# Opening loads reordered and moved to SyncE, first two low parts moved to VectorE, decay tables built at the end of a step, and layer 1's tables loaded in layer 0's down stage

## The chip, the cores and the metric

The kernel runs on one core of a Trainium2 chip. The metric is the device time of one execution in microseconds (us). Three runs of the kernel before took 2464.4, 2457.11 and 2462.2 us, a median of 2462.2 us.

## The reference, cut to what matters

Two blocks are applied one after the other to x of shape (1, 512, 1024), in fp32. The first has two layers, and each layer computes:

```python
proj = x @ w_in[i]                      # q, k, v of both attentions, gates
ya = neighbourhood_attention(q_na, k_na, v_na, na_rpb[i])        # softmax over a 2D window
yb = bidirectional_retention(q_r, k_r, v_r, g_r, decay_f, decay_b)  # decay_in = exp(log_g * |i-j|)
merged = sigmoid(gate_a) * (ya @ w_branch_a[i]) + sigmoid(gate_b) * (yb @ w_branch_b[i])
x = layer_norm(ALPHA * x + merged @ w_out[i], ...)
ffn = conv_glu_ffn(x, w_up[i], conv_w[i], conv_b[i], w_down[i])
ple = sigmoid(x @ w_ple_gate[i]) * (p[i] @ w_ple_proj[i])
x = layer_norm(ALPHA * x + ffn + ple, ...)
```

The second block (one layer, called the mixer here) has a pooling and a state-space branch and a gated feed-forward part. Neither the change nor the rows below touch it, but for small parameters that are loaded at the start.

## The kernel before, in words

**Products in three passes.** Every fp32 operand of a large product is split into a high part (rounded to the matmul's type) and a low part (the rest). Each product is three matmuls: high x high, low x high, high x low (`passes`, line 730 is its matmul). So TensorE does three matmuls of 128x512 per tile of 128x128 weights.

**The weight stream.** All weights lie in one array of units, 8 tiles (512 KB) each, in the order of use. A ring of four slots holds them. For each unit SyncE (SP) loads `stage` (line 355, it waits for `lo_done` of the slot's last user), ScalarE (ACT) copies it to `w_hi` (line 1164 in `round_ahead`, three units ahead of the product, or line 1479 for the first three units), GpSimd (POOL) subtracts to get `w_lo` (line 400). TensorE (PE) waits for `lo_done` in `take_unit` and counts `unit_used` when it is through.

**The opening.** SP issues unit 0, then x in four loads of two feature tiles each (with unit 1 after the first of them), then units 2 and 3. ACT's queue issues first ident, pick, lnp, convp, decay (all counted in `params_in`), lam, log_dt and mpar (lines 1471 to 1475), and then makes `w_hi` and `xh`; VectorE (DVE) makes `xl` (line 2056); POOL makes all low parts. PE waits for all five of `params_in` (line 1140) ahead of its first matmul. After `xh`, ACT forms the logarithm of the decay rates (`decay_a`, lines 1492 to 1496, with two small steps of DVE at 2059 and 2061).

**Layers.** In each layer L, the loads of rope (cosines and sines), delta (position differences) and masks go out from ACT's queue (lines 1499 to 1501) once all of `xl` is made, since they share their place in SBUF with the up stage's buffers `conv_a` and `conv_b`. DVE waits for all three (`tables_in`, line 2065) ahead of its first step. Then come four attention steps, a loop in each engine's program. A step (`attention`) has 12 units: units 0 and 1 together (`first_units`), unit 2, scores of the window attention, unit 3, more scores, and so on. On DVE a step begins with the decay table of its head: lines 1545 to 1550, two tensor_scalar and one tensor_tensor of 128x896, counted in `dterm`; ACT makes its exponential at line 1216, and DVE uses `d_tab` late in the step. Behind the table on DVE come `na_low` (line 1607), which subtracts the rounded queries and keys from PSUM and so frees the two banks of units 0 and 1, `mask_scores` (bias at 1558, masks at 1566), `normalise` (1586) and `rotate` (1593 to 1600, rope). ACT begins a step by issuing the bias load (1207) and with `round_ahead(0)` and the copy of the queries (1181). PE's unit 2 needs the bank of unit 0, so it waits for `na_q_lo`.

After attention come branches, the output projection, a norm, the per-layer-embedding part, up (44 units), down (22 units; `residual_down` adds each of 8 results to z at line 1806) and a second norm (`norm(L, 1)`: mean on PE, centring on DVE at 1729, squares on ACT at 1297). POOL also computes, between its low parts in layer 0's attention, a long series of small steps for the mixer's eigenvalues, beginning with `growth_and_angle`, which waits for lam and log_dt.

The waits that hold a step's begin on DVE, word for word:

```python
            dve.wait_ge(mpar_in, 16)
            for L in range(DEPTH):
                dve.wait_ge(tables_in, L * 48 + 48)
                stand(dve, dve_passed)
                with dve.Fori(0, 4) as t:
                    attention(L, t)
```

## Time and profile before

| | us |
|---|---|
| median of three runs | 2462.2 |
| runs | 2457.11 to 2464.4 |
| the profiled execution, its own time | 2459.35 |
| its span, first to last instruction | 2457.5 |
| PE busy | 2365.7 (96% of the span) |
| POOL busy | 1121.7 (46%) |
| ACT busy | 976.9 (40%) |
| DVE busy | 962.2 (39%) |

The span is cut into stretches in which a different engine ends the wait. The chain of waits says which work ended last; the timeline gives start, length, engine, line and operation of each instruction, and in brackets how long its engine had been idle and what ended that. Of TensorE, the windows give a granted clock: 1.00 is 2.4 GHz, 0.50 is 1.2 GHz, and values between are a mix over the window. A matmul row's length overlaps the next one's, so rates are read from starts.

### The profile page before, as it was taken

How to read it: one execution, taken by the hardware profiler on the slowest of the kernel's cores; microseconds unless marked ns; L12 is line 12 of the kernel's file. 1: busy time of each engine (PE TensorE's matmuls, PEld its weight loads, DVE VectorE, ACT ScalarE, POOL GpSimd, SP SyncE). 2: the span in 40 equal slices, each digit the busy share in tenths (PEclk: the TensorE clock that was granted, in tenths of full speed). 3: DMA queues.
4: the chain of work that ended last, by engine and by line, in shares of the span. 5: the costliest groups of instructions: out<-in, count | busy, mean ns of one | idle time of the engine just before them, and what ended most of it. 6: DMA issues, size and time to landing. Idle time of an engine off the chain costs nothing.

```text
span 2457.5 us, 32539 instructions
## 1 busy us (share of the span) xinstructions
PE 2365.7 (96%) x11792; PEld 1947.2 (79%) x11792; DVE 962.2 (39%) x1487; ACT 976.9 (40%) x1318; POOL 1121.7 (46%) x686
## 2 busy tenths in 40 slices
PE   7999999999999998999999999999999889999998
PEld 5877888878888886788888887888888667888886
DVE  6454453343433203543543234444365594111101
ACT  4343343343555414333434224455521524444321
POOL 5677333444444453233332553444455564444442
PEclk9999999999999998999999999999999899999999
DMA  5212222223232322122222322233233112222331
GB/s 184 75 51 75 83 68 94 95 65 111 90 102 92 105 95 92 61 75 75 75 76 70 103 96 79 89 96 102 94 112 103 52 35 77 94 95 93 103 98 56
DMA packets 60990, 214.12 MB, mean 87 GB/s; under 512 B 7168, under 2 KB 7424, under 8 KB 60928
## 3 DMA queue, kind: packets, MB, share of 16 engines
q1 hardware_dynamic: 56896, 203.45, 25.3%
q10 hardware_dynamic: 4032, 9.81, 1.2%
q8 instruction: 44, 0.72, 0.1%
q14 instruction: 18, 0.15, 0.0%
HBM read 211.13 MB, written 2.10 MB: 87 GB/s over the span
## 4 chain that ended last, share of the span: by engine, by line
PE 87%; DVE 6%; ACT 3%; issue 2%; DMA 1%; POOL 1%; SPq 0%; DVEq 0%; ACTq 0%; POOLq 0%
PE psum L730 83%; PE psum L839 2%; DVE states L1932 1%; DVE s_t L1586 1%; PE psum L826 1%; ACT z L1314 1%; ACT s_t L1194 1%; ACT xh L1313 1%; DMA masks<-in_masks 0%; DMA stage<-in_w 0%; DVE z L1729 0%; PE psum L926 0%; PE psum L941 0%; PE psum L1042 0%; POOL rstd L609 0%
## 5 line engine op out<-in xcount | busy, mean ns | idle before, releaser
L400 POOL TENSOR_TENSOR w_lo<-stage,w_hi 128x1024 fp32r<-128x1024 f32 x380 | 925.8, 2444 | 1269.5 <-ACT w_hi L1164 1258.1
L730 PE MATMUL psum<-xh,w_hi 128*128 128x512 f32 x1888 | 747.2, 396 | 30.5 <-DVE xl L2056 13.3
L730 PE MATMUL psum<-xl,w_hi 128*128 128x512 f32 x1888 | 741.4, 393 | 0.0
L730 PE MATMUL psum<-xh,w_lo 128*128 128x512 f32 x1888 | 740.9, 392 | 0.0
L1164 ACT ACTIVATE w_hi<-stage 128x1024 fp32r<-128x1024 f32 x377 | 396.6, 1053 | 353.5 <-PE psum L730 352.7
L730 PEld LDWEIGHTS psum<-xh,w_hi 128*128 128x128 f32 x1888 | 358.6, 190 | 113.0 <-issue 20.6
L730 PEld LDWEIGHTS psum<-xh,w_lo 128*128 128x128 f32 x1888 | 358.4, 190 | 76.0
L730 PEld LDWEIGHTS psum<-xl,w_hi 128*128 128x128 f32 x1888 | 359.2, 190 | 72.9
L730 PE MATMUL psum<-g_hi,w_hi 128*128 128x512 f32 x528 | 205.4, 389 | 0.0
L730 PE MATMUL psum<-g_lo,w_hi 128*128 128x512 f32 x528 | 205.4, 389 | 0.0
L730 PE MATMUL psum<-g_hi,w_lo 128*128 128x512 f32 x528 | 205.4, 389 | 0.0
L730 PEld LDWEIGHTS psum<-g_hi,w_hi 128*128 128x128 f32 x528 | 99.1, 188 | 20.7
L730 PEld LDWEIGHTS psum<-g_lo,w_hi 128*128 128x128 f32 x528 | 99.1, 188 | 20.5
L730 PEld LDWEIGHTS psum<-g_hi,w_lo 128*128 128x128 f32 x528 | 99.1, 188 | 20.4
L1339 ACT ACTIVATE conv_b<-psum,convp 128x512 f32<-128x512 f32 x44 | 34.3, 779 | 145.6 <-PE psum L730 145.6
L1784 DVE SCALAR_TENSOR_TENSOR conv_b<-psum,convp,conv_b 128x511 f32<-128x511 f32 x44 | 33.0, 749 | 149.2 <-ACT conv_b L1339 149.2
L2030 DVE TENSOR_TENSOR hidden<-psum,silu 128x512 f32<-128x512 f32 x22 | 15.2, 691 | 183.7 <-PE psum L730 183.7
L730 PE MATMUL psum<-w_hi,xh 128*128 128x256 f32 x256 | 74.5, 291 | 4.6 <-DVE r_tmp L1594 4.6
L730 PE MATMUL psum<-merged_p,w_hi 128*128 128x512 f32 x256 | 78.8, 389 | 0.0
L730 PE MATMUL psum<-w_lo,xh 128*128 128x256 f32 x256 | 73.2, 286 | 0.0
L730 PE MATMUL psum<-w_hi,xl 128*128 128x256 f32 x256 | 73.1, 285 | 0.0
L1806 DVE TENSOR_TENSOR z<-z,psum 128x512 f32<-128x512 f32 x16 | 11.0, 687 | 154.6 <-PE psum L730 154.6
(354 smaller groups left out, 3260.3 us busy)
## 6 DMA issues: line engine op xcount, KB each, us to landing
stage<-in_w SPq DMA_DIRECT2D x380, 512.0 KB, 3.5
bias<-in_bias ACTq DMA_DIRECT2D x8, 384.0 KB, 3.1
z<-in_x SPq DMA_DIRECT2D x4, 512.0 KB, 8.5
out_x<-out_t SPq DMA_DIRECT2D x4, 512.0 KB, 2.7
masks<-in_masks ACTq DMA_DIRECT2D x2, 576.0 KB, 5.8
rope<-in_rope ACTq DMA_DIRECT2D x2, 512.0 KB, 3.8
p_raw<-in_p ACTq DMA_DIRECT2D x2, 512.0 KB, 3.6
delta<-in_delta ACTq DMA_DIRECT2D x2, 448.0 KB, 4.5
```

The source lines that it names most:

```text
L400: pool.tensor_tensor(w_lo[s][:, :, :], stage[s][:, :, :], w_hi[s][:, :, :].bitcast(F32), ALU.subtract).then_inc(lo_done, 1)
L730: mm = pe.matmul(dst, lhs[i], rhs[j], start=start and n == 0, stop=stop and n == 2)
L826: mm = pe.transpose(T_BANK[i % 2][:, b * P:(b + 1) * P], s_t[:, i, b * P:(b + 1) * P], ident[:, :])
L839: mm = pe.matmul(dst, na_v[:, j - 1 + b, r0:r0 + NA_DH], pt[:, i % 2, b * P:(b + 1) * P], start=b == bs[0], stop=b == bs[-1])
L1164: act.activation(w_hi[s][:, :, :], stage[s][:, :, :], ACT.Copy).then_inc(hi_done, 1)
L1194: act.activation(s, s, ACT.Exp, bias=row_nmax[:, i:i + 1], accum_out=row_sum[:, i:i + 1])\
L1313: act.activation(xh[:, k, :], p_sig[k % 4][:, :], ACT.Identity, bias=b).then_inc(x_hi, 1)
L1314: act.activation(z[:, k, :], p_sig[k % 4][:, :], ACT.Identity, bias=b).then_inc(x_ready, 1)
L1339: act.activation(buf[c][:, :], U_BANK[half][:, :], ACT.Identity, scale=convp[:, bass.ds(L, 1), 1, ch].rearrange("p l c -> p (l c)"), bias= ...
L1586: dve.tensor_scalar(s, s, row_inv[:, i:i + 1], None, ALU.mult).then_inc(p_ready, 1)
L1784: dve.scalar_tensor_tensor(out=y[:, 1:T], in0=ps[:, 0:T - 1], scalar=tap(0), in1=y[:, 1:T], op0=ALU.mult, op1=ALU.add).then_inc(conv_left, 1)
L1932: dve.tensor_tensor_scan(x[:, m, :], st[:, 4, 4 * q + m:4 * q + m + 1].to_broadcast([P, NB]), x[:, m, :], 0.0, ALU.mult, ALU.add).then_inc ...
```

## The change

SP now issues every opening load, in this order: unit 0, x tile 0, x tile 1, unit 1, x tiles 2-3, 4-5, 6-7, unit 2, decay, delta, unit 3, ident, pick, masks, rope, lam, log_dt, mpar, lnp, convp. ACT's queue issues none at the start; ACT instead runs a one-element copy as soon as two constants are set. The low parts of units 0 and 1 are made by DVE in place of POOL. The one semaphore for all tables becomes several (delta, masks, cosines and sines, ident with pick, decay), each waited for where its data is used; PE no longer waits for parameters at its start, and ACT waits for lnp and convp ahead of its first attention step. The decay table is made by a function `decay_table`: for layer 0's first step ahead of the loop, for later steps at the end of the step before, and for layer 1's first step inside layer 0's down stage, into a buffer of its own over `xl`, from where ACT copies it to `d_tab` at the start of the norm. DVE's loop over steps runs three times and the fourth step is written out behind it. Layer 1's delta, masks and rope are loaded by ACT's queue at the start of layer 0's down stage, once the last low part of the up stage's result (`g_lo`) is there.

```diff
@@ -174,6 +174,8 @@
         d_tab = place("d_tab", [P, 7 * P])
+        d_next = place("d_next", [P, 7 * P], offset=z_at - 4096)
+        d_next_tmp = place("d_next_tmp", [P, 7 * P], offset=z_at - 8192)
@@ -354,13 +357,29 @@
+            def load_x(i, first, end):
+                sp.dma_start(z[:, first:end, :], a["x"][:, first:end, :]).then_inc(x_in[i], 16)
+
             load(0, 0)
-            for h in range(4):
-                sp.dma_start(z[:, 2 * h:2 * h + 2, :], a["x"][:, 2 * h:2 * h + 2, :]).then_inc(x_in[h], 16)
-                if h == 0:
-                    load(1, 1)
+            load_x(0, 0, 1)
+            load_x(1, 1, 2)
+            load(1, 1)
+            for h in range(1, 4):
+                load_x(1 + h, 2 * h, 2 * h + 2)
             load(2, 2)
+            sp.dma_start(decay[:], a["decay"]).then_inc(decay_in, 16)
+            sp.dma_start(delta[:, :], a["delta"]).then_inc(delta_in, 16)
             load(3, 3)
+            for dst, src in ((ident, "ident"), (pick, "pick")):
+                sp.dma_start(dst[:], a[src]).then_inc(pe_params_in, 16)
+            sp.dma_start(masks[:, :, :], a["masks"]).then_inc(masks_in, 16)
+            sp.dma_start(rope[:, :, :], a["rope"]).then_inc(cos_sin_in, 16)
+            sp.dma_start(lam[:, :, :], a["lam"]).then_inc(lam_in, 16)
+            sp.dma_start(dt[:, 0, :], a["log_dt"]).then_inc(lam_in, 16)
+            sp.dma_start(mpar[:, :], a["mpar"]).then_inc(mpar_in, 16)
+            for dst, src in ((lnp, "lnp"), (convp, "convp")):
+                sp.dma_start(dst[:], a[src]).then_inc(params_in, 16)
+
@@ -581,7 +600,8 @@
-            low_parts(0, 4)
+            pool.wait_ge(lo_done, 2)
+            low_parts(2, 4)
@@ -811,6 +831,7 @@
                     pe.wait_ge(o_norm, it * 4 + 4)
+                    pe.wait_ge(pe_params_in, 32)
@@ -1137,8 +1158,7 @@
             pe.sem_inc(unit_used, 1)
-            pe.wait_ge(params_in, 16 * 5)
-            pe.wait_ge(consts_set, 3)
+            pe.wait_ge(consts_set, 4)
@@ -1213,6 +1233,8 @@
                 act.wait_ge(dterm, it * 3 + 3)
+                if L:
+                    act.wait_ge(dtab_moved, L)
@@ -1290,6 +1312,10 @@
                 to_mixer = n == DEPTH * 2 - 1
+                if which and not to_mixer:
+                    act.wait_ge(dterm, (L * 4 + 4) * 3 + 3)
+                    act.wait_ge(mean_done, n + 1)
+                    act.activation(d_tab[:, :], d_next[:, :], ACT.Copy).then_inc(dtab_moved, 1)
@@ -1468,11 +1494,8 @@
             act.sem_inc(bank_free[1], 1)
-            for dst, src in ((ident, "ident"), (pick, "pick"), (lnp, "lnp"), (convp, "convp"), (decay, "decay")):
-                act.dma_start(dst[:], a[src]).then_inc(params_in, 16)
-            act.dma_start(lam[:, :, :], a["lam"]).then_inc(lam_in, 16)
-            act.dma_start(dt[:, 0, :], a["log_dt"]).then_inc(lam_in, 16)
-            act.dma_start(mpar[:, :], a["mpar"]).then_inc(mpar_in, 16)
+            act.wait_ge(consts_set, 2)
+            act.activation(warm[:, :], ln_eps[:, :], ACT.Copy)
@@ -1480,14 +1503,14 @@
             for k in range(KT):
-                if k % 2 == 0:
-                    act.wait_ge(x_in[k // 2], 16)
+                if k < 2 or k % 2 == 0:
+                    act.wait_ge(x_in[k if k < 2 else 1 + k // 2], 16)
                 act.activation(xh[:, k, :], z[:, k, :], ACT.Copy).then_inc(x_hi, 1)
-                if k == 1:
+                if k == 0:
-            act.wait_ge(params_in, 16 * 5)
+            act.wait_ge(decay_in, 16)
@@ -1496,9 +1519,8 @@
                 act.wait_ge(x_lo, (L * 2 + 1) * KT)
-                act.dma_start(rope[:, :, :], a["rope"]).then_inc(tables_in, 16)
-                act.dma_start(delta[:, :], a["delta"]).then_inc(tables_in, 16)
-                act.dma_start(masks[:, :, :], a["masks"]).then_inc(tables_in, 16)
+                if L == 0:
+                    act.wait_ge(params_in, 32)
@@ -1518,6 +1540,11 @@
                     act.dma_start(c_st[:], a["c_st"]).then_inc(c_in, 16)
+                else:
+                    act.wait_ge(g_lo_s, (L + 1) * FT)
+                    act.dma_start(delta[:, :], a["delta"]).then_inc(delta_in, 16)
+                    act.dma_start(masks[:, :, :], a["masks"]).then_inc(masks_in, 16)
+                    act.dma_start(rope[:, :, :], a["rope"]).then_inc(cos_sin_in, 16)
@@ -1533,14 +1560,7 @@
-            def attention(L, t):
-                it = L * 4 + t
-                ui, ri = t * 12, t * 6
-
-                def after_score(n):
-
-                    return s_free[n % 2], it * 6 + (n // 2 + 2)
-
+            def decay_table(it, d_tab, d_tmp):
@@ -1548,6 +1568,15 @@
                 dve.tensor_tensor(d_tab[:, :], d_tab[:, :], d_tmp[:, :], ALU.subtract).then_inc(dterm, 1)
+
+            def attention(L, t, last=False):
+                it = L * 4 + t
+                ui, ri = t * 12, t * 6
+
+                def after_score(n):
+
+                    return s_free[n % 2], it * 6 + (n // 2 + 2)
+
@@ -1612,9 +1641,11 @@
                 na_low(1, na_k, 1.0)
+                dve.wait_ge(masks_in, L * 16 + 16)
                 mask_scores(1)
+                dve.wait_ge(cos_sin_in, L * 16 + 16)
@@ -1676,6 +1707,8 @@
                                       sg[:, f, :], ALU.mult).then_inc(ot_read, 1)
+                if not last:
+                    decay_table(it + 1, d_tab, d_tmp)
@@ -1804,6 +1837,9 @@
                     dve.tensor_tensor(z[:, m, :], z[:, m, :], U_BANK[m % 2][:, :], ALU.add).then_inc(bank_free[m % 2], 1)
+                    if L < DEPTH - 1 and m == 1:
+                        dve.wait_ge(delta_in, L * 16 + 32)
+                        decay_table(L * 4 + 4, d_next, d_next_tmp)
@@ -2047,11 +2083,20 @@
             dve.sem_inc(o_norm, 4)
+            dve.memset(ln_eps[:, :], LN_EPS).then_inc(consts_set, 1)
+            dve.memset(warm[:, :], 0.0).then_inc(consts_set, 1)
             dve.memset(mean_w[:, :], 1.0 / D).then_inc(consts_set, 1)
-            dve.memset(ln_eps[:, :], LN_EPS).then_inc(consts_set, 1)
             dve.memset(rms_eps[:, :], RMS_EPS).then_inc(rms_set, 1)
+
+            def first_low(n):
+                dve.wait_ge(hi_done, n + 1)
+                dve.tensor_tensor(w_lo[n][:, :, :], stage[n][:, :, :], w_hi[n][:, :, :].bitcast(F32), ALU.subtract).then_inc(lo_done, 1)
+
+            first_low(0)
             for k in range(KT):
+                if k == 1:
+                    first_low(1)
@@ -2060,15 +2105,18 @@
             dve.wait_ge(decay_step, 5)
-            dve.wait_ge(mpar_in, 16)
             for L in range(DEPTH):
-                dve.wait_ge(tables_in, L * 48 + 48)
                 stand(dve, dve_passed)
-                with dve.Fori(0, 4) as t:
+                if L == 0:
+                    dve.wait_ge(delta_in, 16)
+                    decay_table(0, d_tab, d_tmp)
+                with dve.Fori(0, 3) as t:
                     attention(L, t)
+                attention(L, 3, last=True)
                     branches(L, i)
+                dve.wait_ge(mpar_in, 16)
```

Left out of it: the semaphores that are declared, and unchanged lines.

## Rows read from the trace of the kernel before

**Rows 1.** The page, chain that ended last: shares of the span by engine.

```profile
PE 87%; DVE 6%; ACT 3%; issue 2%; DMA 1%; POOL 1%; SPq 0%; DVEq 0%; ACTq 0%; POOLq 0%
```

**Rows 2.** The chain of waits in order of time: start us, us, what.

```profile
27.61 6.81 PE psum L730 x30
...
973.79 5.54 DMA masks<-in_masks
...
987.29 8.84 PE psum L730 x30
```

**Rows 3.** Timeline at the start of layer 1.

```profile
971.21 1.63 DVE L1740 SCALAR_TENSOR_TENSOR xl<-p_sig,lnp,xh 128x512 fp32r<-128x512 f32 x2
...
974.57 0.35 ACTq L1207 DMA_DIRECT2D bias<-in_bias  x1
...
977.33 0.58 ACT L1181 ACTIVATE na_q<-psum 128x512 fp32r<-128x512 f32 x1
...
979.91 2.72 DVE L1547 TENSOR_SCALAR d_tmp<-delta,small 128x896 f32<-128x896 f32 x1
...
987.29 0.79 PE L730 MATMUL psum<-xh,w_hi 128*128 128x512 f32 x1 [10.25 <-DVE na_q_lo L1607]
```

**Rows 4.** Timeline of the opening: start us, us, engine line, work xcount [idle before <-releaser].

```profile
2.27 0.62 ACTq L1472 DMA_DIRECT2D convp<-in_convp  x1
...
2.92 0.52 ACTq L1472 DMA_DIRECT2D decay<-in_decay  x1
...
6.40 1.06 ACT L1479 ACTIVATE w_hi<-stage 128x1024 fp32r<-128x1024 f32 x1
...
13.29 0.77 PE L730 MATMUL psum<-xh,w_hi 128*128 128x512 f32 x1 [13.29 <-DVE xl L2056]
...
18.63 0.37 ACTq L1207 DMA_DIRECT2D bias<-in_bias  x1
...
24.09 0.20 DVE L1545 COPY small<-decay 128x2 f32 x1 [4.81 <-DMA masks<-in_masks]
...
25.07 0.60 ACT L1181 ACTIVATE na_q<-psum 128x512 fp32r<-128x512 f32 x1 [3.55 <-PE psum L730]
...
25.66 1.09 DVE L1550 TENSOR_TENSOR d_tab<-d_tab,d_tmp 128x896 f32<-128x896 f32 x1
...
26.68 0.88 DVE L1607 SCALAR_TENSOR_TENSOR na_q_lo<-psum,na_q 128x128 fp32r<-128x128 f32 x4
...
27.61 0.50 PE L730 MATMUL psum<-xh,w_hi 128*128 128x512 f32 x1 [0.53 <-DVE na_q_lo L1607]
```

**Rows 5.** DMA issues, whole kernel: what, queue, count, size, median us to landing.

```profile
stage<-in_w SPq DMA_DIRECT2D x380, 512.0 KB, 3.5
...
convp<-in_convp ACTq DMA_DIRECT2D x1, 176.0 KB, 9.2
...
decay<-in_decay ACTq DMA_DIRECT2D x1, 8.0 KB, 9.9
```

**Rows 6.** Windows of the opening: us, busy us of five engines, PEclk, DMA share, GB/s.

```profile
8.00:18.50 10.50, 5.21 (x12) 4.13 (x13) 9.15 (x9) 7.88 (x13) 6.83 (x3) 1.00 1.05 386
...
18.60:27.00 8.40, 8.40 (x37) 6.66 (x35) 3.49 (x8) 3.89 (x4) 5.34 (x8) 1.00 0.93 342
```

**Rows 7.** Timeline of layer 0's down stage and of the norm behind it.

```profile
835.94 1.99 ACT L1164 ACTIVATE w_hi<-stage 128x1024 fp32r<-128x1024 f32 x2
...
860.25 0.69 DVE L1806 TENSOR_TENSOR z<-z,psum 128x512 f32<-128x512 f32 x1 [14.28 <-PE psum L730]
...
952.63 1.82 ACT L1297 ACTIVATE sq<-z 128x512 f32<-128x512 f32 x3 [6.95 <-DVE z L1729]
```

**Rows 8.** Windows over three of the eight steps' softmax stretches (first, fifth, last).

```profile
46.00:62.00 16.00, 15.45 (x78) 13.22 (x79) 14.86 (x27) 6.49 (x15) 7.85 (x5) 0.79 0.20 67
...
1005.00:1020.00 15.00, 14.02 (x92) 12.25 (x90) 14.39 (x27) 6.83 (x16) 5.43 (x3) 1.00 0.22 72
...
1277.00:1292.00 15.00, 14.01 (x65) 11.52 (x64) 13.31 (x27) 6.68 (x17) 3.38 (x3) 0.77 0.21 70
```

More of the change, by code:

```diff
@@ L267, in build @@
         params_in = sem("params_in")
-        x_in = [sem(f"x_in{i}") for i in range(4)]
+        x_in = [sem(f"x_in{i}") for i in range(5)]
         consts_set = sem("consts_set")
@@ L271, in build @@
         decay_step = sem("decay_step")
-        tables_in = sem("tables_in")
+        delta_in, masks_in, cos_sin_in = sem("delta_in"), sem("masks_in"), sem("cos_sin_in")
+        pe_params_in, decay_in = sem("ident_and_pick_in"), sem("decay_in")
         bias_in = sem("bias_in")
@@ L276, in build @@
         vt_done, v_ready = sem("v_turned"), sem("v_ready")
-        dterm_copy = sem("decay_rates_copied")
+        dterm_copy, dtab_moved = sem("decay_rates_copied"), sem("decay_table_moved")
         dterm, dtab_ready = sem("decay_terms"), sem("decay_table_ready")
```

## The prediction, made before the changed kernel ran

> **What bounds the kernel now.** I read the chain of waits first. PE carries 87% of the span [rows 1], so time can only come from places where PE waits or runs at the lower of its two clock levels. In order of time the chain leaves PE for a long piece of DMA twice, and layer 1's piece is the load of the masks, 5.54 us, behind which a group of 30 matmuls takes 8.84 us; the same group takes 6.81 us at 27.61 [rows 2]. So a matmul costs 6.81/30 = 0.227 us at 2.4 GHz, and the group at 987.29 lost 2.03 us to 1.2 GHz after a pause.
>
> Then I read the timeline at both places. In layer 1, PE ends its first pair of units at 987.29 - 10.25 = 977.04 and stands for 10.25 us until DVE's `na_q_lo` frees the bank [rows 3]. ACT had the queries ready at 977.33, but DVE first waited for masks (973.79 + 5.54 = 979.3) and then made the decay table, whose first operation took 2.72 us with POOL at work. In layer 0 the same wait on DVE lasted 4.81 us, but PE lost only 0.53 us by it, since its first pair ended at 27.61 - 0.53 = 27.08; there the loss is in front: the first matmul is at 13.29, although `w_hi` of unit 0 was begun at 6.40 [rows 4]. The release is put down to `xl`, but the last of the five parameters, decay, landed at 2.92 + 9.9 = 12.8 [rows 4, 5], and that is what PE waited for. The opening's DMA runs at 386 and 342 GB/s with a busy share near 1 [rows 6]: it is bandwidth-bound.
>
> **Layer 1's tables, the main term.** The three issues on ACT go; with them the bias load is issued at about 972.9, when the last `xl` is done (971.21 + 1.63 = 972.8), not 974.57. From that issue to the query copy it was 977.33 - 974.57 = 2.76 us, so the copy comes at 975.7. PE's unit 0 is by then through (nine matmuls before 977.04, 975.0). The copy is 0.58; from the start of `na_q_lo` to PE's matmul it was 27.61 - 26.68 = 0.93 [rows 4]. With 0.05 between, unit 2 starts at 977.25 instead of 987.29: 10.04 us. The pause is now 0.2 us, so the clock stays up: 2.03 more. Sum 12.07. Masks and bias are needed only after unit 2.
>
> Price of the move. In the down stage ACT's wait for `g_lo` and three issues (0.35 to 0.6 each, as ACT's row of 0.62 for convp [rows 4]) put off `w_hi` at 835.94 by up to 2 us; three units of 24 x 0.227 = 5.4 us lie between it and its use, so PE covers it. DVE's table comes behind the addition at 860.25, with 14.28 us of idle time before each such addition [rows 7]; even at 2.72 for each tensor_scalar, and 1.09 for the third [rows 3, 4], it is 6.7 us and is hidden; without that cover it would cost 6.7. The 2.72 is what DVE pays beside POOL's subtraction. The Trainium skill, GPSIMD Engine Reference, Specifications, says that GpSimd's SBUF interfaces are shared with VectorE, against instructions in a two-port mode or with two SBUF inputs; the trace agrees for this table, and by that rule the copies at the opening are safe only because POOL is idle then. ACT's copy of the table, between 0.9 and 1.06 us (a 128x1024 copy [rows 4]), begins when the mean is done, 0.7 before the first square at 952.63 could start: the squares are put off by about 0.2 us, bounds 0 and 1.1.
>
> **The opening.** Unit 0 alone would land 3.5 us after issue at 0.73, at 4.2; I take 4.5 (upper bound 6.4, where its copy started [rows 4]). ACT's table load is out of the way by then. Copy 1.06, low part on DVE 1.25 (1.09 for 896 columns [rows 4], scaled to 1024), `xl` 0.7: PE's first three matmuls at 7.5. Two x tiles and unit 1, 1.05 MB at 386 GB/s, land at 7.2; copy 8.3, low part 9.5, next `xl` 10.2. The first pair took 27.08 - 13.29 = 13.8 us; with the break of 10.2 - 8.8 = 1.4 it ends at 22.7, 4.4 earlier. (The clock column says 1.00 there, but 48 matmuls at 0.227 would be 10.9; the starts show the lower level at first.)
>
> But ACT now waits for lnp and convp, the last of 20 loads on SP's queue, ahead of its bias load and its next `w_hi`. All 6.66 MB lie before it: 6.14 MB behind unit 0, at 386 to 342 GB/s 15.9 to 18.0 us, landing at 20.4 to 22.5 [rows 6]; I take 21.5. Then 0.3 into the loop, 2.76 to the query copy, 0.63 and 0.93 as above: unit 2 starts at 26.1 instead of 27.61. Gain 1.5; bounds 2.6 and, if convp lands at 23, 0. DVE's first table is done by then: log rates after unit 2's copy, about 17.5, and 2.9 of work. PE then idles 3.4 us between 22.7 and 26.1, and may run the next unit at the lower level: up to 2.0 lost, the size seen in layer 1. Against it DVE's softmax part of this step may escape POOL's low parts, up to 2 us gained. I take both together as zero. Everything that makes POOL start later (it gets lam later, and `w_hi` 3 later) is covered by PE's need of unit 4 only some 20 us on.
>
> **Steps.** The table at a step's end stands at the same place in DVE's order as at the next step's start: nothing. Waits added inside the steps (masks, cosines on DVE, ident on PE) are satisfied; at 0.02 to 0.07 each on the path, 16 of them cost 0.3 to 1.1; I take 0.5.
>
> **Sum.** 12.07 + 1.5 - 0.2 - 0.5 = 12.9 us. Against the profiled execution's own 2459.35 that is 2446.5; against the median, 2.85 higher, 2449.3. The mean of the four times known (three runs and the profiled one) is 2460.8, which gives 2447.9, my forecast. A measurement of this kernel can tell about 0.3% (7.4 us) from no change.
>
> **The clock as an unknown.** Behind each step's softmax PE pauses for some us; the granted clock over the eight stretches is 0.79 in the first, 1.00 in the fifth and 0.77 in the last [rows 8]. (1 - clock) x length is the time lost: 3.4, 0 and 3.4 in these. Since the change shifts all phases, each stretch may be drawn anew, so the fifth may lose 3.4 and the others gain. I take zero, +-3 for the range.
>
> **Rivals.**
> A. Small loads hold the queue. convp landed at 2.27 + 9.2 = 11.5 and decay, of 8 KB, at 12.8: 1.3 us for almost no bytes [rows 4, 5]. That was with a second queue taking turns; if it also holds on one queue, four such loads (decay, log_dt, mpar, lnp) add 5.2 us in place of the 1.1 that I left: convp at 25.6, unit 2 at 30.2, a loss of 2.6 instead of 1.5 gained, and 2.0 for the clock after 7.5 us of pause. 2447.9 + 6.1 = 2454.0. The Trainium skill, DMA: Bandwidth & Descriptors, Rules for kernel authors, says of transfers under 64 KB that one pays mostly overhead, which is this rival; no row shows it for one queue alone.
> B. The next wait takes the place. The load that ends ahead of unit 2 in layer 1 is not masks but ACT's order, or the stretches fall to the lower clock: if all eight lose 3.4, against about 13.5 now (mean 1.7), 13.7 is given back and the result is 2461.6, no change. For it: half the stretches show it now. Against it: all eight would have to.
> C. Slower. DVE's fourth step is written out, so its code is fetched afresh in both layers. If DVE must wait for its instructions, each time for a load as long as a landing here (3.5 us for one on a free queue [rows 5]), four times in each of two copies, while PE waits on it, that is 28 us: 2476. It decides above four such waits in all (12.9/3.5). Nothing in DVE's waits now shows one, and its straight-line code in the down stage and norms runs without any.
> D. The opening gives more (convp early, softmax free of POOL, clock kept): 3 to 4 us, 2444.
> E. The change doesn't do what it says: layer 1's wait stays since the tables come late. They have over 100 us between the down stage's start and use, so hardly.
>
> **Chances.** Forecast within 2444 to 2452: 0.62; A 0.13; B 0.10 (most of it partly, 2453 to 2458); C 0.03; D 0.11; E 0.01. The range to hold 8 in 10 reaches into A and D: 2443 to 2456. Faster by over 0.3% (below 2454.8) needs the forecast, D, most of A: 0.83. Same 0.14, slower 0.03.
>
> **What would show it.** Right: layer 1's unit 2 within 1 us of the end of the first pair, no DMA piece in the chain there, the decay table at about 861, and ACT's copy between mean and squares; PE's first matmul near 7.5, unit 2 near 26 with ACT's wait for convp as what ended last. Wrong: a new idle time of PE above 5 us behind the first pair of layer 0 (A); DVE idle on "issue" in a fourth step (C); granted clock below 0.85 in most stretches (B); or layer 1's pause shortened by less than 8 us.

## The result, and the profile after

The changed kernel took 2445.5 us, the median of four runs (2443.96 to 2447.06), beside 2460.1 us for the kernel before (four runs, 2457.11 to 2464.4): a ratio of 0.9931 with a 95% interval of 0.9916 to 0.9945. Run again, as **c_after** below, it was 2447.15 us beside 2463.3, at 0.9932 (0.9918 to 0.9945). (The ratio isn't the quotient of the two medians, which is 0.9941 here and 0.9934 for c_after. A gain in us that is worked out from ratios therefore differs by some us from one worked out from medians, and both are given where it matters.) The forecast was 2447.9 us with a range of 2443.0 to 2456.0. The profiled execution took 2447.06 us (span 2445.3), so against the 2459.35 us of the profile before 12.3 us went.

The page of the changed kernel, busy times and the chain by engine:

```profile
PE 2366.5 (97%) x11792; PEld 1947.1 (80%) x11792; DVE 957.5 (39%) x1490; ACT 977.6 (40%) x1320; POOL 1117.3 (46%) x684
...
PE 89%; DVE 6%; ACT 2%; issue 2%; POOL 1%; SPq 0%; DMA 0%; DVEq 0%; ACTq 0%; POOLq 0%
```

PE does the same work, and its share of the chain rose from 87% [rows 1] to 89%: what left is waiting. The chain in order of time shows where (start us, us, what); the groups of 120 and of 1590 matmuls, one per step and one per layer, serve as markers below:

```profile
12.20 8.90 DMA convp<-in_convp
...
25.83 6.81 PE psum L750 x30
...
81.35 22.34 PE psum L750 x120
...
588.51 360.76 PE psum L750 x1590
...
963.48 20.39 PE psum L750 x78
...
1027.88 22.34 PE psum L750 x120
```

At the start of layer 1, where [rows 2] had the masks' DMA and then a slow group of 30, there is one unbroken group of 78 matmuls: the first pair's 48 and unit 2's 30. The timeline there:

```profile
972.53 0.35 ACTq L1227 DMA_DIRECT2D bias<-in_bias  x1
973.03 1.28 ACT L1184 ACT_TABLE_LOAD   x1 [1.06 <-DVE xl L1773]
...
975.36 0.60 ACT L1201 ACTIVATE na_q<-psum 128x512 fp32r<-128x512 f32 x1
...
975.99 0.88 DVE L1636 SCALAR_TENSOR_TENSOR na_q_lo<-psum,na_q 128x128 fp32r<-128x128 f32 x4 [3.85 <-ACT na_q L1201]
```

DVE now stands ready for 3.85 us and waits for ACT's query copy; the bank is free at 976.9, and the first pair ends only at 963.48 + 20.39 - 6.81 = 977.06. [rows 3] had 10.25 us of idle PE here.

The markers of both profiles, each the start of its group, give the 12.2 us by place:

| stretch | before | after | gained |
|---|---|---|---|
| start to layer 0's first x120 | 83.46 | 81.35 | 2.11 |
| layer 0's first to fourth x120 | 280.81 | 281.03 | -0.22 |
| from there to its x1590 | 224.97 | 226.13 | -1.16 |
| to layer 1's first matmul | 374.94 | 374.97 | -0.03 |
| to layer 1's first x120 | 75.99 | 64.40 | 11.59 |
| layer 1's first to fourth x120 | 275.06 | 275.15 | -0.09 |

So in these two profiles layer 1's start carries the change, the opening adds two microseconds, and the stretch with the norm in the middle of layer 0 gives one back.

The opening after, by the timeline:

```profile
4.48 1.06 ACT L1502 ACTIVATE w_hi<-stage 128x1024 fp32r<-128x1024 f32 x1 [2.10 <-DMA stage<-in_w]
...
5.57 1.22 DVE L2094 TENSOR_TENSOR w_lo<-stage,w_hi 128x1024 fp32r<-128x1024 f32 x1 [4.13 <-ACT w_hi L1502]
...
7.54 0.77 PE L750 MATMUL psum<-xh,w_hi 128*128 128x512 f32 x1 [7.54 <-DVE xl L2101]
...
11.18 0.79 PE L750 MATMUL psum<-xh,w_hi 128*128 128x512 f32 x1 [2.02 <-DVE xl L2101]
...
16.89 0.43 PE L750 MATMUL psum<-xl,w_hi 128*128 128x512 f32 x1
...
22.02 1.28 ACT L1184 ACT_TABLE_LOAD   x1 [5.77 <-DMA convp<-in_convp]
23.32 1.06 ACT L1184 ACTIVATE w_hi<-stage 128x1024 fp32r<-128x1024 f32 x1
24.28 0.58 ACT L1201 ACTIVATE na_q<-psum 128x512 fp32r<-128x512 f32 x1
...
25.83 0.50 PE L750 MATMUL psum<-xh,w_hi 128*128 128x512 f32 x1 [1.45 <-DVE na_q_lo L1636]
```

PE starts 5.75 us earlier than in [rows 4] (7.54 for 13.29), but unit 2 only 1.78 us earlier (25.83 for 27.61): ACT stands 5.77 us for convp, the last of SP's loads, which was issued at 12.20 and landed at 21.1. At 2.4 GHz a matmul starts 0.23 us after the one before; here they start 0.43 apart, which is 1.2 GHz, and the row at 16.89 is the first of the faster ones. The pause of 2.02 us ends with the second tile of `xl`, which ACT and DVE make only behind unit 1's high and low parts. The clock column reads 1.00 all the same (us, busy us of PE, PEld, DVE, ACT and POOL, clock, DMA share, GB/s), so it can't be trusted at the start of the program:

```profile
7.50:17.00 9.50, 7.43 (x17) 5.39 (x18) 6.15 (x9) 7.74 (x13) 2.46 (x1) 1.00 1.03 403
```

The down stage and the norm behind it:

```profile
834.70 0.35 ACTq L1545 DMA_DIRECT2D delta<-in_delta  x1
...
835.57 0.45 ACTq L1547 DMA_DIRECT2D rope<-in_rope  x1
836.13 2.01 ACT L1184 ACTIVATE w_hi<-stage 128x1024 fp32r<-128x1024 f32 x2 [0.79 <-issue]
...
859.55 0.69 DVE L1839 TENSOR_TENSOR z<-z,psum 128x512 f32<-128x512 f32 x1 [14.27 <-PE psum L750]
...
860.48 0.69 DVE L1567 TENSOR_SCALAR d_next_tmp<-delta,small 128x896 f32<-128x896 f32 x1
...
951.27 0.95 ACT L1318 ACTIVATE d_tab<-d_next 128x896 f32<-128x896 f32 x1 [6.29 <-PE psum L942]
```

The moved pieces are there (the masks' issue, at 835.08, lies between the two shown). PE loses nothing by them: `z` at 859.55 is 0.70 ahead of 860.25 [rows 7], and layer 1's first matmul is 0.70 ahead of 964.18 too, with the issues behind it and the table and the copy between.

### The profile page after: what moved, and what is told of

It is laid out like the page before. It is cut to its first block, busy times and chain, and to the rows that moved or that the text cites. A ratio compares the mean times of both kernels' runs of the same rounds, so it can differ in the third digit from the quotient of the medians.

```text
span 2445.3 us, 32512 instructions
## 1 busy us (share of the span) xinstructions
PE 2366.5 (97%) x11792; PEld 1947.1 (80%) x11792; DVE 957.5 (39%) x1490; ACT 977.6 (40%) x1320; POOL 1117.3 (46%) x684
## 4 chain that ended last, share of the span: by engine, by line
PE 89%; DVE 6%; ACT 2%; issue 2%; POOL 1%; SPq 0%; DMA 0%; DVEq 0%; ACTq 0%; POOLq 0%
PE psum L750 84%; PE psum L860 2%; DVE s_t L1615 1%; DVE states L1968 1%; PE psum L847 1%; ACT s_t L1214 1%; PE psum L947 1%; ACT z L1340 0%; DVE z L1762 0%; ACT xh L1339 0%; PE psum L962 0%; DMA convp<-in_convp 0%; PE psum L1063 0%; POOL rstd L629 0%; POOL w_lo L419 0%
## 6 DMA issues: line engine op xcount, KB each, us to landing
masks<-in_masks SPq DMA_DIRECT2D x1, 576.0 KB, 10.6
```

## The experiments

The kernels below the changed one ran in four batches, each beside the kernel before on the same chip, whose medians were 2462.6 (e1 to e4), 2463.3 (c_after, e5, e6, e7_pool_order), 2464.3 (e7_again, e8, e9_pool_alone) and 2462.8 us (e9_again). "First step" is the start of layer 0's first x120, "layer 1" the time from its first matmul to its first x120, both from the one profiled execution.

| kernel | median us (range, runs) | ratio [95%] | first step | layer 1 |
|---|---|---|---|---|
| before | | | 83.46 | 75.99 |
| changed | 2445.49 (2443.96-2447.06, 4) | 0.9931 [0.9916, 0.9945] | 81.35 | 64.40 |
| c_after | 2447.15 (2445.02-2450.04, 5) | 0.9932 [0.9918, 0.9945] | 84.67 | 64.26 |
| e1_opening_only | 2458.1 (2452.71-2463.7, 12) | 0.9988 [0.9977, 0.9998] | 80.24 | 77.12 |
| e2_tables_only | 2451.2 (2448.67-2453.06, 5) | 0.9958 [0.9945, 0.9971] | 85.83 | 64.18 |
| e3_table_at_start | 2450.03 (2446.84-2451.48, 5) | 0.9946 [0.9933, 0.9958] | 85.37 | 64.44 |
| e4_params_late | 2445.02 (2443.9-2447.44, 5) | 0.9932 [0.992, 0.9945] | 79.44 | 64.32 |
| e5_warm | 2444.04 (2443.42-2447.4, 5) | 0.9925 [0.9911, 0.9939] | 80.46 | 64.26 |
| e6_hold | 2444.37 (one run) | | 80.32 | 64.22 |
| e7_pool_order | 2446.71 (2441.29-2447.63, 5) | 0.9929 [0.9915, 0.9942] | 74.33 | 65.81 |
| e7_again | 2442.7 (2438.31-2447.49, 5) | 0.992 [0.9907, 0.9933] | 74.26 | 64.25 |
| e8_all | 2441.53 (2438.96-2447.42, 6) | 0.991 [0.9896, 0.9924] | 81.10 | 64.24 |
| e9_pool_alone | 2442.68 (2440.78-2445.55, 4) | 0.9909 [0.9895, 0.9923] | 77.64 | 65.75 |
| e9_again | 2441.77 (2441.36-2446.97, 5) | 0.992 [0.9907, 0.9934] | 84.29 | 64.25 |

### The two halves of the change

**e1_opening_only** is the changed kernel with layer 1 as before: its three loads go out at its start again, DVE waits for them and makes the table there.

```diff
-                if which and not to_mixer:
...
-                    act.activation(d_tab[:, :], d_next[:, :], ACT.Copy).then_inc(dtab_moved, 1)
+                else:
+                    act.dma_start(rope[:, :, :], a["rope"]).then_inc(cos_sin_in, 16)
...
-                    act.wait_ge(g_lo_s, (L + 1) * FT)
...
-                    if L < DEPTH - 1 and m == 1:
-                        dve.wait_ge(delta_in, L * 16 + 32)
-                        decay_table(L * 4 + 4, d_next, d_next_tmp)
...
+                    dve.wait_ge(masks_in, L * 16 + 16)
+                decay_table(L * 4, d_tab, d_tmp)
```

> The changed kernel with layer 1 as before: rope, delta and masks are loaded at layer 1's start, DVE waits for all three there and makes the table there. Theory (two independent gains, 2.1 us in the opening and 11.6 us at layer 1's start): about 2 us faster than the kernel before, PE's unit 2 in layer 0 at 25.8, and in layer 1 again a pause of about 10 us behind the first pair. Rival (the opening's order pays in other places, or the gains overlap): more than 5 us faster, or a pause in layer 1 under 8 us.

Its chain at layer 1:

```profile
971.33 6.40 DMA masks<-in_masks
...
979.76 2.72 DVE d_tmp L1560
...
985.05 9.72 PE psum L750 x30
```

The wait of [rows 2, 3] is back, with the slow group of 30 behind it (9.72 us), and layer 1 takes 77.12 us. The opening alone is worth a ratio of 0.9988, about 3 us (4.5 by the medians), with an interval that nearly reaches no change.

**e2_tables_only** is the kernel before with layer 1's part alone: the loads in the down stage, the table at `m == 1`, the copy in the norm, the tables at a step's end.

```diff
+                if which and not to_mixer:
+                    act.wait_ge(dterm, (L * 4 + 4) * 3 + 3)
+                    act.wait_ge(mean_done, n + 1)
+                    act.activation(d_tab[:, :], d_next[:, :], ACT.Copy).then_inc(dtab_moved, 1)
...
+                else:
+                    act.wait_ge(g_lo_s, (L + 1) * FT)
+                    act.dma_start(delta[:, :], a["delta"]).then_inc(tables_in, 16)
...
-                with dve.Fori(0, 4) as t:
+                if L == 0:
+                    decay_table(0, d_tab, d_tmp)
+                with dve.Fori(0, 3) as t:
+                attention(L, 3, last=True)
```

> The kernel before with only layer 1's part: tables loaded in layer 0's down stage, table of layer 1's first step made there, steps' tables at the end of the step before, DVE's fourth step written out. Theory: 10 to 12 us faster than before, layer 0's opening unchanged (first matmul 13.3, unit 2 at 27.6), no pause behind layer 1's first pair. Rival (written-out step or the added waits cost something that the opening hides): under 9 us faster.

Layer 1 takes 64.18 us as in the changed kernel, and the ratio is 0.9958, 10.3 us. The two halves together make 3.0 + 10.3 = 13.3 us where the whole has 0.0069 x 2460 = 17.0; the intervals (+-2.6, +-3.2 and +-3.6 us) leave room for simple addition. By the medians it is 4.5 + 11.4 = 15.9 us beside 14.6 and 16.2. Its opening shows what DVE's common wait could cost there (chain):

```profile
20.03 6.10 DMA masks<-in_masks
...
29.84 2.34 PE psum L733 x9
```

Its opening code is that of the kernel before, but its masks landed at 26.1 and its unit 2 came at 29.84, not 27.61 [rows 4]. So the same opening moves by 2 us between two profiles.

### Which part of layer 1's half counts

**e3_table_at_start** loads early but makes the table at layer 1's start, without `d_next` and the copy.

```diff
-                    act.activation(d_tab[:, :], d_next[:, :], ACT.Copy).then_inc(dtab_moved, 1)
...
-                        decay_table(L * 4 + 4, d_next, d_next_tmp)
...
-                if L == 0:
-                    dve.wait_ge(delta_in, 16)
-                    decay_table(0, d_tab, d_tmp)
+                dve.wait_ge(delta_in, L * 16 + 16)
+                decay_table(L * 4, d_tab, d_tmp)
```

> The changed kernel, but layer 1's first decay table is made at layer 1's start from the delta loaded early; no extra buffer, no copy on ACT. Theory (the loads are nearly all of it): DVE starts the table at about 972.2, ahead of POOL's low part at 975.5, and needs 2.9 us, so the queries' low part starts at most 0.3 us late: same as the changed kernel within 1 us. Rival (the table made ahead carries a part of the gain, since beside POOL a tensor_scalar took 2.7): up to 4 us slower than the changed kernel, with a pause of 3 to 4 us behind the first pair.

```profile
976.26 0.69 DVE L1561 TENSOR_SCALAR d_tmp<-delta,small 128x896 f32<-128x896 f32 x1
...
977.58 1.09 DVE L1564 TENSOR_TENSOR d_tab<-d_tab,d_tmp 128x896 f32<-128x896 f32 x1
979.94 0.88 DVE L1630 SCALAR_TENSOR_TENSOR na_q_lo<-psum,na_q 128x128 fp32r<-128x128 f32 x4 [1.27 <-ACT na_q L1201]
```

The table is ready at 978.7 and DVE still waits 1.27 us for the query copy. Its first operation takes 0.69 us, not 2.72 as in [rows 3]: POOL's subtraction begins only at 979.47, behind the table. Layer 1 takes 64.44 us. For this stretch, making the table ahead is worth nothing once the loads are early; the loads' move is the whole of the 11.6 us. (The build's times were expected within 1 us of the changed kernel's, and its ratio of 0.9946 lies 3 to 4 us above. Its first step ended at 85.37 in the profile, and nothing in its layer 1 gives a cause; what the rest of the difference is stays open.)

### The opening: what bounds it

**e4_params_late** lets ACT wait for lnp and convp behind layer 0's attention. **e5_warm** adds 14 matmuls on a constant tile, into a bank not yet used, ahead of PE's first unit. **e6_hold** is the changed kernel with PE held until unit 1's low part is made.

```diff
-                if L == 0:
-                    act.wait_ge(params_in, 32)
                 with act.Fori(0, 4) as t:
                     attention(L, t)
+                if L == 0:
+                    act.wait_ge(params_in, 32)
```

e5, beside that edit, and e6, which has this line alone:

```diff
+            for n in range(14):
+                pe.matmul(O_BANK[:, 0:P], mean_w[:, :], mean_w[:, :], start=True, stop=True)
```

```diff
+            pe.wait_ge(lo_done, 2)
```

> The changed kernel, but ACT waits for lnp and convp behind layer 0's attention instead of ahead of it. Theory (that wait, ended by convp's landing at 21.1, is what holds unit 2 at 25.8): ACT's bias load goes out at about 16.5 and the copy of the queries waits for PE; unit 2 starts right behind the first pair, at about 24.5, 1.3 us earlier; total 1 to 2 us faster than the changed kernel (14 to 16 faster than before). Rival (bias load and first high part then collide with the opening's transfers or clock phases eat it): same as the changed kernel within 0.5 us, with unit 2 still after 25.3.

In e4 the bias load is issued at 15.10 (21.47 in the changed kernel), and unit 2 starts right behind the first pair, at 22.98 instead of 25.83. So ACT's wait for convp is what held unit 2. But it cost PE only its 1.45 us of waiting: the other 1.4 of the 2.85 us are the first pair's end, 22.98 for 24.39. No edit touches the pair; its matmuls behind the pause are at the lower level for 3.15 us here and for 5.71 in the changed kernel. Only 1.9 of the 2.85 us are left at the first x120, and the ratio is the same 0.9932, not the 1 to 2 us that were expected. DVE's timeline beside POOL's shows where a part went; the first row is PE's start of unit 2:

```profile
22.98 0.48 PE L750 MATMUL psum<-xh,w_hi 128*128 128x512 f32 x1
...
31.87 5.26 POOL L419 TENSOR_TENSOR w_lo<-stage,w_hi 128x1024 fp32r<-128x1024 f32 x2
...
32.13 0.42 DVE L1587 TENSOR_TENSOR s_t<-psum,bias 128x256 f32<-128x256 f32 x1
32.47 2.40 DVE L1595 CUSTOM_DVE_ANT_0 s_t<-s_t,masks 128x384 f32<-128x384 f32 x1
```

> The variant with the late parameter wait, and 14 matmuls of a constant tile by itself on PE from the moment the constant is set (about 1.5) until about 7, results unused. Theory (the first pair loses time to the lower clock level until 14 to 17 us, because PE was idle ahead of it and pauses for 2 us in it): the level is up by 7.5 or at least ends before 12, the first pair ends at about 21.5 instead of 22.9, 1 to 2 us gained. Rival (the pause between the third and the fourth matmul, 9.0 to 11.2, brings it down again, or the pair is bound by the arrival of x): first pair ends after 22.5, nothing gained.

```profile
7.52 0.47 PE L750 MATMUL psum<-xh,w_hi 128*128 128x512 f32 x1 [0.54 <-DVE xl L2103]
...
11.47 0.50 PE L750 MATMUL psum<-xh,w_hi 128*128 128x512 f32 x1 [3.02 <-DVE xl L2103]
...
13.13 0.63 PE L750 MATMUL psum<-xh,w_hi 128*128 128x512 f32 x1
```

The first three matmuls run at full rate, but 1.3 us behind the 3 us of waiting for the second tile of `xl` the level falls, at 12.72, and stays low to 16.12. The first pair ends at 23.42, not at the 21.5 of the theory, and the first x120 gains nothing over e4 (80.46 for 79.44). The rival holds.

> The changed kernel, but PE waits for unit 1's low part (about 10.5) ahead of its first matmul, so it starts at about 11 without a pause. Theory (three matmuls ahead of a 2 us pause neither raise the clock nor are worth more than their own 1.3 us, and the wait for convp covers that): first pair ends up to 1.3 us later, unit 2 unchanged at about 25.8. Rival (the early start is worth its 4 us): unit 2 later by over 1 us.

```profile
11.02 0.77 PE L750 MATMUL psum<-xh,w_hi 128*128 128x512 f32 x1 [11.02 <-DVE w_lo L2095]
...
14.15 0.41 PE L750 MATMUL psum<-xl,w_hi 128*128 128x512 f32 x1
```

Held back by 3.5 us, PE runs without a pause, is at full rate after 3.1 us, and ends the first pair at 23.66, earlier than the changed kernel's 24.39. Unit 2 starts at 25.96 against 25.83, since convp holds it. So the early start of PE, for which the two low parts went to DVE, brings unit 2 nothing as long as ACT waits for convp. What it does to the pair itself is not settled by this one run. In the seven profiles with the early start and no matmuls ahead of it in which the pair's end can be read (changed, c_after, e1, e3, e4 and both of e9) PE is at the lower level for 2.7 to 5.7 us behind the pause, and the pair ends between 22.98 and 24.39, on both sides of e6's 23.66. Nor are the 3.1 us a rule for a start without a pause: in the kernel before it was 5.66 us.

**c_after** is the changed kernel again.

> The changed kernel once more, beside the others of this set. 14 to 17 us faster than before. Theory (the first step of layer 0 has a length of its own in each execution, by what POOL's low parts and the clock do to it): its first group of 120 matmuls starts between 80 and 86, while the stretch from layer 1's first matmul to its group of 120 is 64.4 again within 0.3.

Layer 1's 64.26 repeats the changed kernel's 64.40, but its first x120 is at 84.67 instead of 81.35, from the same code. Two things took the time. Unit 2 starts 0.4 us later and is at the lower level from 26.20 to 29.72, so that DVE's mask work begins 2.0 us later (34.15 for 32.15). And POOL's subtractions fall on the mask rows:

```profile
37.13 0.41 DVE L1587 TENSOR_TENSOR s_t<-psum,bias 128x256 f32<-128x256 f32 x1
37.36 5.08 POOL L419 TENSOR_TENSOR w_lo<-stage,w_hi 128x1024 fp32r<-128x1024 f32 x2
37.47 2.71 DVE L1595 CUSTOM_DVE_ANT_0 s_t<-s_t,masks 128x384 f32<-128x384 f32 x1
...
40.11 2.61 DVE L1595 CUSTOM_DVE_ANT_0 s_t<-s_t,masks 128x256 f32<-128x256 f32 x1
```

Each mask row, 0.41 to 0.58 us when POOL is idle, lasts about as long as one of POOL's subtractions (2.54 each): it seems to get its turn only when that is through. In the changed kernel's profile the same two subtractions (37.52 to 42.26) fell 2 us later in DVE's order, on the four scalings of `s_t`, which took 4.04 us for 1.32 without them (in e9_pool_alone, below). The Trainium skill, SBUF — State Buffer, SBUF: two separate sides, calls the port pair of VectorE and GpSimd an exclusive lock, held for a whole instruction by whichever starts first. These rows agree: the row of 2.71 began just behind the first subtraction and the next just behind the start of the second. DVE's additions that read PSUM aren't touched: e4's, at 32.13 in the midst of POOL's 5.26 us, took 0.42.

### Moving POOL's two low parts

In layer 0 POOL made the low parts of units 4 and 5 behind `growth_and_angle`, in the midst of DVE's softmax. **e7_pool_order** (e4 with this edit), **e9_pool_alone** (the changed kernel with this edit alone) and **e8_all** (e7 with e5's matmuls) make them ahead of it.

```diff
-            low_parts(2, 4)
+            low_parts(2, 6)
             growth_and_angle()
-            low_parts(4, 6)
```

> The variant with the late parameter wait, and POOL makes the low parts of units 4 and 5 ahead of its eigenvalue steps instead of behind them. Theory (in layer 0's first step DVE's masks and normalising run beside POOL's low parts of units 4 and 5 at 32 to 37 and take 2.4 to 2.6 instead of 0.6 each, 3 to 4 us on the path): those low parts end by 31, DVE's four mask rows take under 0.7 each, group of 120 matmuls starts 3 to 4 us earlier (about 76), 3 us faster in all than with the late wait alone. Rival (contention only moves to the next operations of the step): under 1 us gained.

> The same kernel as e7_pool_order, to learn how its time is spread. Its profile ended layer 0's first step at 74.33 us, 5.1 us earlier than e4_params_late, but its times were 2441.29, 2442.92, 2446.71, 2447.21 and 2447.63. If the 5 us in the first step are real and a late phase of the clock gate gives some of them back in some runs, the profile again ends that step at 73 to 77 us and the ratio to before is 0.991 to 0.993. If the early end was a chance of one profile, the step ends at 79 to 82 us and the ratio is 0.993 or above.

> e7 with e5's 14 matmuls on constants ahead of the first unit. e5 showed that these bring the first three matmuls to full rate and that the lower level then comes later, with no gain by the end of the first step; so this should be within 1 us of e7_again, ratio 0.991 to 0.993. If in this order the first pair's slow stretch is what bounds the step (POOL no longer in the way), it is 2 us shorter than e7_again and the first step ends 2 us earlier than that one's.

> The changed kernel with one edit alone: POOL makes the low parts of units 4 and 5 ahead of its eigenvalue steps. ACT still waits for the parameters ahead of layer 0's attention. If the vector engine's slow mask rows beside POOL cost the first step its 4 to 5 us, this step ends at 76 to 78 us in place of 81.35, and the ratio is 0.991 to 0.993. If unit 2, which waits for the parameters at 26 us, is the bound of the step, or if it needs both edits, it ends at 80 to 84 us and the ratio is that of the changed kernel, 0.993.

> The kernel of e9_pool_alone once more, which was 2442.68 us at a ratio of 0.9909 [0.9895, 0.9923] where the changed kernel had 0.9931 and 0.9932. If moving POOL's two low parts is worth its 4 us on the mean, the ratio is again 0.990 to 0.992 and the first step ends at 76 to 79 us. If e9_pool_alone was a lucky draw of the clock's phase, the ratio is 0.993.

In e9_pool_alone the subtractions run from 25.28 to 32.37, when DVE has only `na_low` to do, which reads PSUM (0.89 a row), and then waits for PE. Mask rows and scalings are then short:

```profile
25.28 7.09 POOL L419 TENSOR_TENSOR w_lo<-stage,w_hi 128x1024 fp32r<-128x1024 f32 x3 [7.37 <-ACT w_hi L1183]
...
36.57 0.42 DVE L1594 CUSTOM_DVE_ANT_0 s_t<-s_t,masks 128x256 f32<-128x256 f32 x1
...
39.78 1.32 DVE L1614 TENSOR_SCALAR s_t<-s_t,small 128x256 f32<-128x256 f32 x4
```

Its first step ends at 77.64, 3.7 us earlier; with e4's edit beside it, at 74.33 and 74.26. DVE's shorter rows are only a part of this. In all nine profiles with the old order of POOL, those of before and e2 among them, PE's pauses in the first softmax are followed by 2.3 to 5.3 us at the lower level, and the granted clock from 40 to 56 us is 0.68 to 0.89. In the five with the new order it is 1.00, or 0.96 in e8.

That is not yet a dependable gain, since the second softmax part of the step meets POOL in its turn. The four scalings there took 4.10 us in e7_pool_order and 4.11 in e9_pool_alone. In e8_all (7.58; first x120 at 81.10) and in e9_again (first x120 at 84.29, where PE stood 4.5 us at 55 to 59.7) they took more, which for e9_again is the row

```profile
49.22 7.88 POOL L419 TENSOR_TENSOR w_lo<-stage,w_hi 128x1024 fp32r<-128x1024 f32 x3
...
52.59 5.62 DVE L1614 TENSOR_SCALAR s_t<-s_t,small 128x256 f32<-128x256 f32 x4
```

This would explain why e7's five times lie in two groups (2441.29 and 2442.92; 2446.71 to 2447.63), but the trace shows only one execution of each build, both of e7's were of the quicker group, and e9_pool_alone's profile with its 77.64 is the longest of that build's four times (2445.55). So it is not shown. e7's own expectation, a first step 3 to 4 us shorter than e4's and 3 us in all, was more than met in the step (5.1 us) and not in the times of its first build (0.9929 for e4's 0.9932); e7_again has 0.992. The first steps of e8 (expected within 2 us of e7_again's 74.26) and of e9_again (expected at 76 to 79) were misses; their ratios lay where they were expected. Over both builds e9's nine times have a median of 2441.8 us (2440.78 to 2446.97), the changed kernel's nine 2446.4 us (2443.96 to 2450.04). The medians are 4.6 us apart, and the intervals of their ratios still overlap; the three ratios of e9 and e8 (0.9909, 0.992, 0.991) are all below the changed kernel's two. The best version that these runs point to is e9, two lines from the changed kernel.

## Why the prediction was right, and where its terms were off

**Layer 1, 12.07 predicted, 11.59 measured.** The mechanism is the one named. The pause went whole (10.25, not 10.04), since the query copy came at 975.36 and not 975.7. The 2.03 us of the clock came too: the group of 78 runs through at full rate at its end. What was left out is the first pair itself: it was at the lower level until 969.19, for 5.71 us, and in the profile before for 3.57, so it ended 13.58 us after its start and not 12.86. That is 10.25 + 2.03 - 0.72 = 11.56. Over ten of the twelve profiles with early loads the stretch is 64.18 to 64.44 (65.8 in the other two, whose pair ended sooner, so that PE waited 0.23 and 0.61 us for `na_q_lo`; the rest of their 1.5 us isn't traced), against 75.99 and 77.12 with late ones: the best-settled number here.

**The opening, 1.5 predicted, 2.11 measured, by steps that were partly wrong and with luck.** First matmul 7.5 predicted, 7.54 measured; convp 21.5 and 21.1; unit 2 at 26.1 and 25.83, with ACT's wait for convp as the last one: right. The first pair's end, 22.7 predicted, was 24.39. The step that failed here took over the 13.8 us of the kernel before and added 1.4 for a break. The break was 2.01, and behind it PE was at the lower level until 16.89, 7.3 us in all where the kernel before had 5.66 from its start. Nor is that a fixed size: the pair ends at 22.98 in e4 and at 24.39 here. It cost nothing, because convp held unit 2 anyway, as e6 shows from the other side. The last term, clock loss against relief from POOL, was set to zero as a pair. The rows show that neither is steady: after the gap ahead of unit 2 the level stayed up in the changed kernel and fell for 3.5 us in c_after, and POOL's two subtractions cost DVE 4.04 - 1.32 = 2.7 us in the one and 2.71 + 2.61 - 0.55 - 0.42 = 4.4 in the other. The first x120 lies at 80.2 to 85.4 in the five profiles with this opening (changed, c_after, e1, e3, and e6 with its held start). In a range of 5 us, that the one difference of 2.11 lies so near 1.5 is luck; the times say 3.0 us by e1's ratio and 4.5 by its medians.

**ACT's copy, 0.2 predicted, nothing measured** (rows on both sides are ahead by the same 0.70). **The added waits, 0.5 predicted:** the steps of layer 0 and layer 1 are longer by 0.22 and 0.09. That is within what they vary by (280.17 to 281.14 in layer 0 in c_after and e1 to e6), so no run shows a cost, and none bounds it closely. **DVE's table in the down stage** took 0.69 for its first operation, not the 2.72 allowed for; POOL's subtraction had ended at 860.42, just ahead of it, and it was hidden in either case.

**What was not foreseen, 1.16 us** between the attention and the up stage of layer 0: the first matmuls behind its norm ran at 1.2 GHz (530.46 to 532.34), in the profile before at full rate, which is 0.9 of it. No edit touches it, and it isn't of the change: over all fourteen profiles this stretch is 225.0 to 227.5 us, and 225.0 in e5, e7_pool_order, e8 and e9_again too, which have the change.

**The sum.** 12.9 predicted from the profiled execution, 12.3 measured from it. By medians it is 14.6 (first comparison) and 16.2 (c_after), because the profiled execution of before, 2459.35, is 1 to 5 us under the medians of its kernel, and that of the changed kernel, 2447.06, is 1.6 above its own. That the sum comes out so near is in part luck: against the prediction the opening gave 0.6 us more, the copy and the waits cost 0.4 less, layer 1 gave 0.5 less, and 1.2 us were not foreseen. The two profiles of the old opening (first x120 at 83.46 and 85.83) are too few to say what its mean is; this part of the gain stays open.

**The rivals.** A, small loads that hold the queue: refuted. convp landed at 21.1, not 25.6. Eight KB of decay landed 8.8 us after its issue, and masks of 576 KB 10.6 us after theirs: on one queue, behind the same bytes, the size of a load hardly shows.

```profile
masks<-in_masks SPq DMA_DIRECT2D x1, 576.0 KB, 10.6
...
convp<-in_convp SPq DMA_DIRECT2D x1, 176.0 KB, 8.9
...
decay<-in_decay SPq DMA_DIRECT2D x1, 8.0 KB, 8.8
```

This rival would have given 2454.0. The Trainium skill, DMA: Bandwidth & Descriptors, Rules for kernel authors, says of transfers under 64 KB that one pays mostly overhead; this trace does not bear it out for loads that queue behind large ones. B, the clock: the softmax stretches of the first, fifth and last step have 0.79, 1.00 and 0.77, as in [rows 8]. In this profile they weren't drawn anew:

```profile
44.00:60.00 16.00, 15.71 (x79) 13.46 (x80) 14.86 (x26) 6.17 (x15) 11.67 (x9) 0.79 0.27 94
993.00:1008.00 15.00, 14.04 (x91) 12.50 (x92) 14.39 (x27) 6.57 (x16) 5.18 (x3) 1.00 0.24 74
1265.00:1280.00 15.00, 14.15 (x66) 11.78 (x67) 13.18 (x28) 6.65 (x16) 3.35 (x3) 0.77 0.22 70
```

Other executions of the same code are: in c_after layer 1's three steps are 91.6, 91.7 and 91.8 us, in the changed kernel's profile 91.7, 90.1 and 93.3. C, code of the written-out fourth step: refuted; from third to fourth x120 it is 90.17 after 90.15 in layer 0 and 93.34 after 93.23 in layer 1, and from layer 1's fourth x120 to its x1590 225.21 after 225.23. D, the opening gives 3 to 4 us: open, since the profiles say 2.11 and e1's times 3.0 to 4.5. E: the change does what it says. Of its parts in layer 1, only the loads' move shortens the stretch (e3).

## What to carry to other kernels

Look at what each engine has queued behind a wait that it doesn't need itself: here DVE's one common wait for three tables kept from PE a bank that needed none of them, and the lower clock level came on top of the pause (2.03 us on 10.25). An early start buys nothing while another wait holds the work behind it: e6 started PE 3.5 us later, and unit 2 came 0.13 us later, with ACT's wait for convp in front of it. And where two profiles of the same code differ by microseconds, put GpSimd's long subtractions beside VectorE's rows that read SBUF alone, and look for an order in which they can't meet.

## What the runs showed of the hardware that was not expected

- VectorE beside a 128x1024 subtraction of GpSimd: mask rows 2.4 to 2.7 us for 0.41 to 0.58, four scalings of 128x256 4.0 to 7.6 us (e8_all) for 1.3, a bias addition that reads PSUM 0.41, unchanged.
- The sixteenth matmul of the opening, 8.9 us after PE's first, was still at 1.2 GHz. With no pause it took 3.1 us to full rate in e6 and 5.66 us in the kernel before. Fourteen small matmuls ahead brought the first three to full rate in e5 and e8; behind the pause that followed, the level fell after 1.3 us in e5 and was down at the first matmul in e8.
- The granted clock column reads 1.00 in the program's first 17 us, while matmuls start 0.43 us apart.
- The steps of one code come in lengths some 1.6 us apart (layer 1's: 90.1, 91.7 and 93.3), about what one more slow stretch costs (c_after's, 26.20 to 29.72 us, 3.52 x 0.47 = 1.7). A difference of that size in one profile is no finding.
